# Sums of squares after an output projection: added up on GpSimd, then summed by TensorE in two matmuls

## The reference

```python
def _rms_norm(x, w, eps=RMS_EPS):
    xf = x.astype(jnp.float32)
    y = xf * lax.rsqrt(jnp.mean(xf * xf, axis=-1, keepdims=True) + eps)
    return (y * w.astype(jnp.float32)).astype(x.dtype)

x = x + _dilated_mixer(_rms_norm(x, b_norm[j]), k_sh, v_sh, att_w_q[j], att_w_o[j], positions)
x = x + _conv_ffn(_rms_norm(x, ffn_norm[layer]), ffn_w_up[layer], ffn_conv_w[layer], ffn_w_down[layer])
```

## Time and profile before

| | |
|---|---|
| median of three runs | 2536.6 us (2529.54, 2536.6, 2542.08) |
| the profiled execution | 2529.77 us, span 2527.9 us |
| granted TensorE clock, mean | 0.953 of full speed |
| PE busy | 2270.4 us (90%) |
| DVE, ACT, POOL busy | 1023.5, 735.4, 227.3 us |

### The profile page before, as it was taken

One profiled execution on the slowest core, in us unless ns is written; L12 is line 12 of the kernel. 1 busy time (PEld: TensorE's weight loads), 2 busy tenths in 40 slices (PEclk: granted clock), 3 DMA queues, 4 the chain that ended last, 5 costly groups with the idle time before them and its releaser, 6 DMA issues. The chain is left out here.

```text
span 2527.9 us, 31841 instructions
## 1 busy us (share of the span) xinstructions
PE 2270.4 (90%) x13732; PEld 1518.7 (60%) x13732; DVE 1023.5 (40%) x1755; ACT 735.4 (29%) x1081; POOL 227.3 (9%) x184
## 2 busy tenths in 40 slices
PE   5886899999999797999999998977999889768998
PEld 2633634444444495444444447955899889658988
DVE  3313421111111364111111116855489565545982
ACT  3122211111111342111111115844354333224541
POOL 0000000000000000000000000156036100001540
PEclk8999899999999898999999998988999999989999
DMA  8712699999999334999999973412345444203642
GB/s 283 250 66 105 248 412 421 421 421 422 412 392 403 130 139 200 381 402 398 398 400 399 401 268 117 167 67 67 125 157 170 167 152 167 100 1 100 198 153 84
DMA packets 197490, 616.90 MB, mean 244 GB/s; under 512 B 19936, under 2 KB 82528, under 8 KB 147936
## 3 DMA queue, kind: packets, MB, share of 16 engines
q1 hardware_dynamic: 190416, 610.96, 63.2%
q10 hardware_dynamic: 6928, 3.81, 0.5%
HBM read 613.69 MB, written 1.05 MB: 243 GB/s over the span
## 5 line engine op out<-in xcount | busy, mean ns | idle before, releaser
L1172 PE MATMUL bank<-ring,arena 128*64 128x512 f32 x2048 | 450.5, 592 | 1.6 <-DVE arena L1531 1.6
L517 PE MATMUL bank<-normed_rounded,ring_rounded 128*128 128x256 f32 (+1 forms) x3368 | 413.3, 285 | 7.4 <-ACT normed_rounded L608 6.4
L517 PEld LDWEIGHTS bank<-normed_rounded,ring_rounded 128*128 128x128 f32 x3368 | 408.4, 190 | 9.7 <-issue 7.2
L294 DVE TENSOR_TENSOR ring_rounded<-ring,ring_rounded 128x4096 fp32r<-128x4096 f32 (+1 forms) x74 | 327.1, 4425 | 162.2 <-ACT ring_rounded L288 162.0
L517 PE MATMUL bank<-arena_rounded,ring_rounded 128*128 128x256 f32 (+1 forms) x2416 | 330.5, 296 | 15.0 <-ACT ring_rounded L288 5.8
L517 PEld LDWEIGHTS bank<-arena_rounded,ring_rounded 128*128 128x128 f32 x2416 | 311.1, 196 | 26.6 <-ACT ring_rounded L288 6.3
L1172 PEld LDWEIGHTS bank<-ring,arena 128*64 128x64 f32 x2048 | 147.5, 137 | 292.8 <-issue 290.7
L288 ACT ACTIVATE ring_rounded<-ring 128x4096 fp32r<-128x4096 f32 (+1 forms) x74 | 259.8, 3515 | 78.2 <-DMA ring<-in_ffn_w_down 53.6
L1536 DVE TENSOR_TENSOR arena<-arena,bank 64x512 f32<-64x512 f32 x64 | 43.5, 680 | 578.4 <-ACT arena L1368 578.4
L1181 PE MATMUL bank<-ring,arena 128*64 128x512 f32 x1024 | 233.9, 599 | 0.0
L505 PEld LDWEIGHTS bank<-mats,arena 128*128 128x128 f32 (+1 forms) x932 | 120.8, 182 | 112.8 <-issue 85.9
(11 more groups left out here) (239 smaller groups left out, 2085.7 us busy)
## 6 DMA issues: line engine op xcount, KB each, us to landing
ring<-in_moe_w_gate SPq DMA_DIRECT2D x128, 1024.0 KB, 8.8
ring<-in_moe_w_up SPq DMA_DIRECT2D x128, 1024.0 KB, 10.9
ring<-in_moe_w_down SPq DMA_DIRECT2D x128, 1024.0 KB, 8.1
ring<-in_w_mod SPq DMA_DIRECT2D x24, 2048.0 KB, 12.5
ring<-in_ffn_w_up SPq DMA_DIRECT2D x44, 1024.0 KB, 7.7
ring<-in_ssm_w_in SPq DMA_DIRECT2D x12, 2048.0 KB, 8.1
ring<-in_ffn_w_down SPq DMA_DIRECT2D x10, 2048.0 KB, 7.8
ring<-in_conv_w_in SPq DMA_DIRECT2D x6, 2048.0 KB, 9.2
```

The lines of the kernel that those rows point to most:

```text
L294: e.tensor_tensor(ring.rounded[slot][:, 0:n].bitcast(F32R), ring.slots[slot][:, 0:n], ring.rounded[(self.number + 1) % RING][:, 0:n], ALU. ...
L517: end = e.matmul(out, lhs.bitcast(F32R), rhs.bitcast(F32R), start=start and n == 0 and k == 0, stop=stop and n == 2 and k == n_k - 1)
L1172: ends[i] = e.matmul(bank[rows, :], self.xt[x][:, j, n * cap:(n + 1) * cap], weights[:, j, :], start=n == 0 and j == 0, stop=n == 1 and j ...
```

## The change

A new class `PooledSquares` takes the place of `Squares` in the six stages named above. ACT squares as before into two buffers, but waits for POOL instead of PE before it reuses one. POOL adds the squares of tiles 0 to 6 in six adds, the first of buffers 0 and 1, the others in place into `total`. PE has only two sums at the end: of the total, when POOL's last add is done, and of the square of tile 7. `total` is 256 columns of a buffer that is free then or newly taken. The methods that call `open_tensor` and `tile_tensor` are as they were; `tile_tensor` does nothing unless it is the last tile. The result is the same but for the order of additions.

```diff
+class PooledSquares(Squares):
+    def __init__(self, k, name, T, buffers, total):
+        super().__init__(k, name, T, buffers)
+        self.total = total
+
+    def square_scalar(self, e, w, n, value, ready):
+        k = self.k
+        w.wait_ge(*ready)
+        if n >= 2:
+            w.wait_ge(*k.pool.at("added", self.name, max(1, n - 2)))
+        e.activation(self.buffers[n % 2], value, ACT.Square).then_inc(*k.act.up("square", self.name, n))
+
+    def add_gpsimd(self, e, w):
+        k = self.k
+        for n in range(1, KD - 1):
+            w.wait_ge(*k.act.at("square", self.name, n))
+            if n > 1:
+                w.wait_ge(*k.pool.now())
+            e.tensor_tensor(self.total, self.total if n > 1 else self.buffers[0], self.buffers[n % 2], ALU.add
+                            ).then_inc(*k.pool.up("added", self.name, n))
+
+    def tile_tensor(self, e, w, n, final):
+        k = self.k
+        if final:
+            bank = k.banks.of("mean", self.name)[:, 0:self.T]
+            w.wait_ge(*k.pool.at("added", self.name, n - 1))
+            e.matmul(bank, k.mat(f"ones_{D}"), self.total, start=True, stop=False)
+            w.wait_ge(*k.act.at("square", self.name, n))
+            e.matmul(bank, k.mat(f"ones_{D}"), self.buffers[n % 2], start=False, stop=True
+                     ).then_inc(*k.pe.up("sums", self.name))
+            k.banks.drop("mean", self.name)
...
-        self.squares = Squares(k, "conv out", SEQ, [k.rstd[:, 0:SEQ], k.rstd[:, SEQ:]])
+        self.squares = PooledSquares(k, "conv out", SEQ, [k.rstd[:, 0:SEQ], k.rstd[:, SEQ:]], ar.take(SEQ))
...
         e.memset(self.V, 0.0).then_inc(*k.pool.up("conv pads"))
+        self.squares.add_gpsimd(e, w)
         k.pool.mark("end", "conv")
```

More of the change, by code:

```diff
@@ L737, in __init__ @@
         self.w_o = [k.weights(("w_o", n), a["mla_w_o"][0], KD, n * 512, 512) for n in range(2)]
-        self.squares = Squares(k, "mla out", SEQ, [tables_both[:, 0:SEQ], tables_both[:, SEQ:2 * SEQ]])
+        self.squares = PooledSquares(k, "mla out", SEQ, [tables_both[:, 0:SEQ], tables_both[:, SEQ:2 * SEQ]], k.rstd[:, SEQ:])
         self.turned = k.rstd[:, 0:SEQ]
@@ L1910, in __init__ @@
         self.w_out = [k.weights(("ssm out", n), a["ssm_w_out_2"][0], 16, n * 256, 256) for n in range(4)]
-        self.squares = Squares(k, "ssm out", SEQ, [k.rstd[:, 0:SEQ], k.rstd[:, SEQ:]])
+        self.squares = PooledSquares(k, "ssm out", SEQ, [k.rstd[:, 0:SEQ], k.rstd[:, SEQ:]], ar.take(SEQ))
     def prepare_scalar(self, e, w):
@@ L2495, in __init__ @@
         self.x_parts = k.parts_of_A()
-        self.squares = Squares(k, ("ffn out", layer), SEQ, [k.rstd[:, 0:SEQ], k.rstd[:, SEQ:]])
+        self.squares = PooledSquares(k, ("ffn out", layer), SEQ, [k.rstd[:, 0:SEQ], k.rstd[:, SEQ:]], ar.take(SEQ))
     def prepare_scalar(self, e, w):
@@ L2677, in __init__ @@
         self.w_o = [k.weights(("att_w_o", n), a["att_w_o_2"][0], KD, n * 512, 512) for n in range(2)]
-        self.squares = Squares(k, "dilated out", SEQ, [k.rstd[:, 0:SEQ], k.rstd[:, SEQ:]])
+        self.squares = PooledSquares(k, "dilated out", SEQ, [k.rstd[:, 0:SEQ], k.rstd[:, SEQ:]], self.S[0][:, 0:SEQ])
         scale = float(ATT_D) ** -0.5
```

## The result

The changed kernel took 2504.6 us (median of four runs, 2503.7 to 2511.3) against 2533.3 of before on the same chip (four runs, 2529.5 to 2542.1): ratio 0.9885, 95% interval 0.9865 to 0.9904. The prediction was 2507.3. Timed again later beside other kernels, after took 2502.1 us (five runs, 2501.1 to 2511.1), ratio 0.9888 (0.9867 to 0.9910).

A forecast was written before the change was run, and what follows sets the result against it. PE, busy 2270.4 of 2527.9 us, bounds the kernel. Gains of MLA 7.5, conv 4.8, SSM 2.6, FFN 0 4.7, dilated 7.1 and FFN 1 2.6 make 29.3 us: profile 2500.5, median 2507.3 (6.8 above), range 2496 to 2521.

The forecast's parts named there:

- Sums, 0.43 us each: All six stages: six sums fewer on PE, 2.6 us a stage, 15.5 us in all.
- its 4.8: Conv: forecast gain of 4.8 us, 2.2 for the gap and 2.6 for the sums.
- Gaps and clock of MLA and the dilated attention: PE's waits and the low clock behind them go; with the sums, MLA gains 7.5 us and dilated 7.1.
- the prediction's own steps, from 2308.6 to 2301.3: Dilated's end: the last sum starts near 2301.3 in place of 2308.6, after the total waits 0.9 us.
- FFN 0, the step that failed: FFN 0 before tile 2: a gap of about 2.2 us stays, the clock is kept, gain 4.7 us.
- the other bound (3.05): FFN 0: gain from the shorter gap and fewer sums, without the 1.7 us for a kept clock.
- POOL's adds at nothing: Six POOL adds a stage cost nothing, at most 0.4 us in each of the two FFNs.
- the rival's break-even of "about 3.3 us an add": Slower rival, POOL locked out by DVE (chance 0.04): whole gain gone at about 3.3 us an add.
- middling adds: Rival: POOL adds of 1.6 to 2 us lengthen FFN and dilated tails, 2512 to 2518 us; chance 0.08.
- MoE passes the gain on: MoE stages behind MLA and conv: their gains pass through; rival that they are swallowed, 2519.6 us, chance 0.06.
- the prediction's own sign (an expert 7 us earlier): MoE in the profile after: prediction is wrong if the first expert does not come 7 us earlier.
- The sum: Six stages' gains together: 29.3 us, for a profiled execution of 2500.5 us and a median of 2507.3.

The follow-up runs named there:

- e2: Kernel before with the pooled sums only in MLA and conv, all other stages unchanged: 2520.3 us, ratio 0.9952 to the kernel before.
- after_timed: The changed kernel, unaltered, timed and profiled once more beside other kernels: 2502.1 us, ratio 0.9888 to the kernel before.
- e1: Changed kernel, but PE still waits for each tile's square where the sums had stood: 2525.4 us, ratio 0.9966 to the kernel before.
- e6: Kernel before with squares pooled in FFN 0 alone: 2532.2 us, ratio 0.9998 to the kernel before.
- e4: Changed kernel with the FFNs' mean bank opened behind all output products: 2503.7 us, ratio 0.9882 to the kernel before; repeated, 2502.1 us, 0.9876.
- e5: Changed kernel, but FFN 0 keeps its eight separate sums on PE: 2508.9 us, ratio 0.9918 to the kernel before.
- e3_adds_x3: Changed kernel with three POOL steps per tile in place of one add: 2529.9 us, ratio 0.9994 to the kernel before.
- after_again: The changed kernel, unaltered, profiled a second time: 2511.8 us in one run.

## Why the prediction was right, and where its terms were off

- *Sums, 0.43 us each.* SSM, which had no gap, gained 2.59 and FFN 1 2.56, where 6 x 0.43 = 2.6 stood. (FFN 1 agrees less closely than it seems: in e2, where its code is that of before, it took 25.93, 1.0 less.) In conv a tile with its sum took 3.26 us in before and 24 products take 2.85 in the other profiles of after, so a sum cost 0.41 there. That conv (5.74) beat its 4.8 is luck: the 0.9 us are the quicker pace of products in one profile. By after_timed conv gained 4.86.
- *Gaps and clock of MLA and the dilated attention.* 7.5 forecast, 7.76 measured; 7.1 forecast, 7.32 measured (the prediction's own steps, from 2308.6 to 2301.3, give 7.3). The total's wait in the dilated attention, 0.9 forecast, was 0.77. e1 shows gap and clock apart from the sums. That the dilated attention's clock stays up was right for the end of the stage (1.00 above); its start runs faster or slower by chance, 23.1 or 25.6 in profiles of one kernel. e6, whose dilated attention is that of before, had the fast kind: 30.41, again 7.3 above 23.1.
- *FFN 0, the step that failed.* The gap was forecast well (2.2, measured 2.12), and the clock was taken as kept because conv's 2.2 us gap had kept it. It fell: 5.2 us at 0.67, 1.7 us. The stage gained 3.14, the other bound (3.05), not 4.7. It fell in all seven profiles in which PE stood 2.1 to 2.3 us there. e4 shows the two parts by taking the gap away. Conv was a poor model in two ways. In before its products ran at 0.50 ahead of the gap, which made them late and the gap short:

```profile
944.10:947.40 3.30, 3.30 (x17) 3.30 (x17) 0.56 (x1) 2.71 (x1) 0.00 (x0) 0.50 0.00 0
```

And the same code in e6, at 1.00 ahead of it, stood 3.69 us for the same sum, with 0.50 behind:

```profile
958.72 1.22 PE L417 MATMUL bank<-rstd,mats 128*128 128x256 f32 x2 [3.69 <-ACT rstd L406]
```

```profile
958.30:961.60 3.30, 2.88 (x11) 2.70 (x12) 0.31 (x1) 0.76 (x2) 0.00 (x0) 0.50 0.00 0
```

The length of the gap alone doesn't decide it either: in e1 PE stood 2.60 us at FFN 0's place (in e5 2.78), and the stretch behind ran at 1.00:

```profile
2035.00:2040.00 5.00, 5.00 (x42) 5.00 (x43) 1.27 (x3) 1.01 (x4) 2.20 (x3) 1.00 0.35 127
```

- *POOL's adds at nothing.* Right: 0.73 to 0.75 us, PE waited for POOL 1.5 us in all, in three stages. But the rival's break-even of "about 3.3 us an add" was wrong. The cover was counted as six tiles of products, 17.1 us; it is what is left between square 1 and the total, 13.0 in MLA. In FFN 0 and FFN 1, where 8.6 had been counted, it is 9.2 and 7.3 (16.86 - 5.6 - 2.1 and 24.39 - 15.0 - 2.1), and the dilated attention's three late adds, priced under "middling adds", had been left out of it. At 2.5 us an add nothing was left (e3_adds_x3). The margin was smaller than stated.
- *MoE passes the gain on.* Right, by e2. By the prediction's own sign (an expert 7 us earlier) it missed in the profile: 6.1, since MLA's projection had begun 1.9 later.
- *The sum.* Projections 29.1 us of 29.3 forecast. That it is so near is partly luck: conv's 0.9 too much and small surpluses in MLA and the dilated attention stand against FFN 0's 1.6 too little. By the other two profiles of after it is 29.7 and 30.6. Between the profiles 24.6 us, between the medians 28.7. The median of before, 6.8 above its profile, carried over as 2507.3; after's own medians were 2504.6 and 2502.1, near its profile, which had been forecast at 2500.5 and took 2505.2. So the profile came out 4.7 above its forecast and the median 2.7 below: that the median is so near is helped by the 6.8 carried over, which is chance. Two profiles of the same kernel end 10.7 us apart (spans of 2499.3 and 2510.0): 3.0 ahead of MLA's projection, 4.1 in the attention behind FFN 0, 2.5 in its projection.

## What to carry to other kernels

A small matmul in PE's queue that waits for another engine also costs its wait and the low clock behind it: in MLA 5.1 us, beside 2.65 for the six sums themselves. Move the reduction to where nobody waits, and leave PE only the matmuls at the end. To know how slow the added step may be, count from the moment the first input is ready to the moment the result is asked for, not from the first tile; and compare each stage by itself, since the rest of the profile moves by some us from run to run.

## What the runs showed of the hardware that I had not expected

- The clock behind a gap isn't told by the gap's length: 2.12 us (FFN 0, after) and 3.33 (MLA, e1) were followed by a stretch at 0.67 and 0.66; 2.60 (FFN 0, e1) and 2.17 (conv) by 1.00. Nor by the code: in FFN 0 2.71 us were followed by 0.65 in before, 2.78 by 1.00 in e5; in the dilated attention 3.08 by 0.56 in before, 3.09 by 1.00 in e6. What decides is open.
- The clock behind a gap goes with what PE did before it: behind FFN 0's mean, with the same gap of 6.2 to 6.4 us, it stays at 0.50 for 3.4 to 3.9 us or for 5.8 to 6.7, and the first 96 products take 13.5 to 13.7 us or 14.6 to 14.9, by how FFN 0 ended. So a gain in a projection can be paid back in part by the next stage.
- The same code ahead of MLA's projection ends at 261.4 to 261.6, 263.2 to 263.5 or 266.0 to 266.7 us in fourteen profiles, in three groups. PE is busy equally long (130.45 and 130.46 us from 93 to 261 in before and after_again), at a clock of 1.00 and 0.94 from 93 to 150 us. What decides between them is open. Both profiles of before lie in the first group and only one of the twelve others does, so that the changed kernels begin later more often isn't excluded; the medians (28.7 us of gain, 29.1 in the projections) don't show it.
